# GpSimd makes the low part of each weight block in eight instructions of 256 columns in place of four of 512

## What is computed

```
h = rms_norm(x, norm1_g)
proj = h @ w_in                      # q, ckv, qi, ki, wi, u, v, ga, gb
y_a = sparse_attention(...) @ w_proj_a
y_b = chunked_gmlp(u, v, ...) @ w_proj_b
x = x + (sigmoid(ga) * y_a + sigmoid(gb) * y_b) @ w_out
x = rms_norm(x + hier_moe(rms_norm(x, norm2_g), ...))
```

```
h = x
for i in range(2):
    h = h + (dilated_mixer, forgetting_mixer)[i](rmsnorm(h, norm[i]), ...)
    h = h + swiglu(rmsnorm(h, ffn_norm[i]), w_gu[i], w_down[i])
out = rmsnorm(h, final_norm)
```

## Time and profile before

| | |
|---|---|
| timed runs | 2390.17 to 2391.84 us, median 2390.87 |
| profiled execution | 2387.72 us |
| its span, first to last instruction | 2385.9 us |
| TensorE, matmuls | busy 2263.3 us, 95% |
| TensorE, weight loads | busy 1907.7 us, 80% |
| VectorE | busy 1365.1 us, 57% |
| ScalarE | busy 1111.8 us, 47% |
| GpSimd | busy 870.3 us, 36% |
| mean granted clock of TensorE | 0.993 |

### The profile page before, as it was taken

One profiled execution on the slowest core, in us unless ns is written; L12 is line 12 of the kernel. 1 busy time (PEld: TensorE's weight loads), 2 busy tenths in 40 slices (PEclk: granted clock), 3 DMA queues, 4 the chain that ended last, 5 costly groups with the idle time before them and its releaser, 6 DMA issues.

```text
span 2385.9 us, 34966 instructions
## 1 busy us (share of the span) xinstructions
PE 2263.3 (95%) x13066; PEld 1907.7 (80%) x13066; DVE 1365.1 (57%) x2171; ACT 1111.8 (47%) x2028; POOL 870.3 (36%) x677
## 2 busy tenths in 40 slices
PE   7999999878888999999998889999999999899998
PEld 6886786545456998899987779999978887899997
DVE  4377445989885232363335687777511124977775
ACT  3344533656664344353343454444444444544443
POOL 4441241546552433333332153333132222533330
PEclk9999999999999999999999999999999999999999
DMA  5521046999994322312322123323232212233232
GB/s 182 173 71 54 36 149 240 343 392 400 392 354 161 105 89 93 103 54 71 104 79 86 36 89 108 106 95 101 89 110 86 71 54 63 80 106 96 99 107 80
DMA packets 164990, 316.68 MB, mean 133 GB/s; under 512 B 19872, under 2 KB 100512, under 8 KB 154992
## 3 DMA queue, kind: packets, MB, share of 16 engines
q1 hardware_dynamic: 157104, 301.97, 36.2%
q0 software_dynamic: 7744, 12.76, 1.6%
HBM read 300.89 MB, written 22.71 MB: 136 GB/s over the span
## 4 chain that ended last, share of the span: by engine, by line
PE 76%; DVE 8%; DMA 6%; ACT 4%; issue 4%; POOL 1%; SPq 1%; DVEq 0%; ACTq 0%; POOLq 0%
PE bank L952 21%; PE bank L954 20%; PE bank L953 20%; DMA w_ring<-in_w_gate 5%; PE bank L1578 2%; PE bank L1204 2%; PE bank L991 2%; PE bank L1183 1%; DVE up_low L2801 1%; PE bank L1555 1%; POOL w_low L3458 1%; PE bank L1194 1%; PE bank L1565 1%; PE bank L1392 1%; PE bank L1187 1%
## 5 line engine op out<-in xcount | busy, mean ns | idle before, releaser
L3458 POOL TENSOR_TENSOR w_low<-raw,w_high 128x512 fp32r<-128x512 f32 x324 | 418.1, 1321 | 820.1 <-ACT w_high L1874 788.5
L952 PE MATMUL bank<-h_high,w_high 128*128 128x256 f32 (+1 forms) x1088 | 362.7, 333 | 8.0 <-DVE h_low L2531 5.8
L954 PE MATMUL bank<-h_high,w_low 128*128 128x256 f32 (+1 forms) x1088 | 357.0, 328 | 0.0
L953 PE MATMUL bank<-h_low,w_high 128*128 128x256 f32 (+1 forms) x1088 | 356.5, 328 | 0.0
L952 PE MATMUL bank<-w_high,h_high 128*128 128x512 f32 (+2 forms) x832 | 326.5, 392 | 7.4 <-DVE h_low L2545 2.9
L954 PE MATMUL bank<-w_high,h_low 128*128 128x512 f32 (+2 forms) x832 | 311.1, 374 | 0.0
L953 PE MATMUL bank<-w_low,h_high 128*128 128x512 f32 (+2 forms) x832 | 310.9, 374 | 0.0
L952 PEld LDWEIGHTS bank<-h_high,w_high 128*128 128x128 f32 x1088 | 207.3, 191 | 31.3 <-DVE h_low L2531 10.3
L954 PEld LDWEIGHTS bank<-h_high,w_low 128*128 128x128 f32 x1088 | 207.3, 191 | 18.6
L952 PEld LDWEIGHTS bank<-w_high,h_high 128*128 128x128 f32 x832 | 204.7, 246 | 21.8 <-DVE h_low L2545 4.5
L953 PEld LDWEIGHTS bank<-h_low,w_high 128*128 128x128 f32 x1088 | 207.6, 191 | 15.5
(11 more groups left out here) (424 smaller groups left out, 4728.0 us busy)
## 6 DMA issues: line engine op xcount, KB each, us to landing
raw<-in_a_w_in SPq DMA_DIRECT2D x72, 512.0 KB, 4.6
w_ring<-in_w_gate SPq DMA_DIRECT2D x35, 1024.0 KB, 10.1
w_ring<-in_w_up SPq DMA_DIRECT2D x35, 1024.0 KB, 12.3
w_ring<-in_w_down SPq DMA_DIRECT2D x35, 1024.0 KB, 9.2
raw<-in_ffn_w_gu SPq DMA_DIRECT2D x48, 512.0 KB, 4.4
raw_more<-in_ffn_w_gu SPq DMA_DIRECT2D x40, 512.0 KB, 4.4
raw<-in_ffn_w_down SPq DMA_DIRECT2D x40, 512.0 KB, 4.4
raw<-in_w_in SPq DMA_DIRECT2D x34, 512.0 KB, 4.5
```

What stands on the lines that cost most here:

```text
L952: pe.matmul(out, sta[0], mov[0], start=start, stop=False, skip_group_check=onto)
L953: pe.matmul(out, sta[0], mov[1], start=False, stop=False, skip_group_check=onto)
L954: return pe.matmul(out, sta[1], mov[0], start=False, stop=stop, skip_group_check=onto)
L3458: last = pool.tensor_tensor(out=w_low[:, slot, cols], in0=raw[:, slot, cols], in1=w_high[:, slot, cols].bitcast(F32), op=ALU.subtract)
```

## The change

`split_low` subtracts the same 2048 columns in eight instructions of 256 columns in place of four of 512. `low_done` is still raised once, behind the last of them. `low_quarter` and the sums are not touched.

```diff
@@ -3453,8 +3453,8 @@
             pool.wait_ge(high_done, n + 1)
 
-            for q in range(4):
-                cols = slice(512 * q, 512 * q + 512)
+            for q in range(8):
+                cols = slice(256 * q, 256 * q + 256)
                 last = pool.tensor_tensor(out=w_low[:, slot, cols], in0=raw[:, slot, cols],
                                           in1=w_high[:, slot, cols].bitcast(F32), op=ALU.subtract)
             last.then_inc(low_done, 1)
```

## The result

The changed kernel takes 2395.24 us (median of 22 runs, 2390.06 to 2398.81); the kernel before takes 2390.73 us (22 runs beside them, 2385.76 to 2398.94). The ratio is 1.0019, with a 95% interval of 1.0012 to 1.0026: slower by 4.5 us, between 2.9 and 6.2. The forecast was 2395.8 us, within 2389.5 to 2400.5; the loss stands just inside the 0.2% that a measurement can tell by the forecast's bound, 4.8 us.

The account below looks back on a forecast made before the run. TensorE's work and its holes bound the kernel; GpSimd matters by latency, not throughput. Waits +7.7, queued places +1.1, VectorE's relief -3.2 and the norm -0.7 gave +4.9 on 2390.87: 2395.8 us, range 2389.5 to 2400.5.

Parts of the forecast that it names:

- The price of a start: GpSimd's split: a start costs about a one-column copy's 0.177 us, four more 0.7 us a block; bounds 0.12 and 1.4.
- rival B: Not slower by over 0.2%: VectorE's relief outweighs smaller waits; at 0.54 a block +2.2 us, 2393.1; chance 0.30.
- rival C: A start is half hidden, 0.35 us a block; sum -0.6 us, 2390.3; chance 0.15.
- The waits in the mixer: Dilated mixer: TensorE waits for each GpSimd block's added 0.7 us less its slack; 7.7 us together with places elsewhere.
- Carried along and not caught up: TensorE's delay moves ScalarE's next w_high too, so every block's added time less its slack adds to the total.
- VectorE's relief: At 34 to 39 us, three VectorE instructions wait less for shorter GpSimd instructions; 3.2 us with the clock.
- The hole: TensorE's 1.74 us idle time until 39.30 us, waiting for VectorE; forecast to shrink by 1.5 us.
- The clock's 1.7 us: Half clock from 40.3 to 43.7 us, after TensorE's idle stretch, expected to vanish, saving 1.7 us.
- The norm: Ahead of the second SwiGLU, TensorE waits for VectorE, whose waits for GpSimd shrink; relief 0.7 us.
- Queued places: Additions onto X after the experts and both SwiGLU starts: VectorE waits for GpSimd's queued work; 0.3 + 0.4 + 0.4 = 1.1 us.
- D: GpSimd loses its turn to VectorE eight times a block instead of four; +3 on the forecast, 2398.8 us; chance 0.13.
- E: Relief turns large and a start is free: faster by over 0.2%, 2386 us; chance 0.05.

Follow-up runs that it names:

- Experiments 1: Eight pieces only in the dilated mixer and its output projection, four elsewhere, against the kernel before: 2396.65 us, ratio 1.0020.
- 9: The changed kernel, but with four pieces in the dilated mixer and its output projection: 2388.90 us, ratio 0.9996 to the kernel before.
- experiment 8: Two pieces in the dilated mixer and its output projection, four elsewhere, against the kernel before: 2399.28 us, ratio 1.0037.
- Experiment 10: One piece of 2048 columns for the block at 34 us alone, against the kernel before: 2392.11 us, ratio 1.0002.
- 5: The kernel before, unchanged, profiled and timed again: 2390.29 us, ratio 0.9999.
- 6: The changed kernel, profiled and timed again: 2396.30 us, ratio 1.0023 to the kernel before.
- 11: A third profile of the changed kernel: 2392.14 us in one run.
- 2: Eight pieces for the block at 34 us alone, four elsewhere, against the kernel before: 2390.12 us, ratio 0.9996.
- 7: The kernel before with four calls of unused matmuls filling TensorE's hole at 39 us: 2391.87 us, ratio 0.9999.
- experiment 4: One piece in the dilated mixer and its output projection, eight for the block at 34 us, against the kernel before: 2426.75 us, ratio 1.0151.

## Why the prediction was right

**What bounds the kernel.** Right: POOL's throughput costs nothing and its latency at the mixer does. Experiments 1 and 9 show it from both sides, 5.5 us with eight in the mixer alone and 0.0 without. The forecast's stretch from 738 to 1345 us has grown by 5.2 us without the half clock, where some 7.5 were forecast.

**The price of a start.** Mis-sized, within its bounds: starts lie 1.246 us apart with 512 columns and 0.694 apart with 256 (medians), so a start is 2 x 0.694 - 1.246 = 0.142 us and a column 2.16 ns. The forecast took the copy's 0.177. Four starts give 0.57, and the blocks grew by 0.56, where 0.7 was forecast. The value is that of rival B (0.54), and B's +2.2 for the whole would have been 2 us too low.

The Trainium skill (GPSIMD Engine Reference, 2.1) has about 2.5 cycles per element as the floor for two inputs, which at 1.2 GHz is an estimate of 2.08 ns a column; its section 3.1, which the prediction names for that figure, has about 2.6 measured, an estimate of 2.17. The trace has 2.16. The Trainium skill (GPSIMD Engine Reference, 7) gives about 102 cycles for a small read command; taken once for each start, four more would be rival C, an estimate of 0.34 us a block. The trace has 0.56 and doesn't bear that out.

**The waits in the mixer.** Forecast 6.6 with 0.7 a block; measured 5.5. By the forecast's own count 0.56 a block gives 2.8 + 0.8 + 0.7 + 0.5 = 4.8. Matmul by matmul there are sixteen steps. The five blocks without slack give 2.8, with the one at 993 us, whose slack was 0.35: it gives 0.23, and the one at 1000 then only 0.31. The four with 0.15 and 0.23 give 0.36 to 0.39 each, 1.5 together. The four with 0.42 to 0.45 give 0.18 to 0.20 each, 0.8 together, where 0.5 would follow from their slack; blocks with 0.74 give nothing. Two steps more, 0.17 at 1035 us and 0.32 at 1074, are at no block's first load. They are a second path, which the forecast didn't have in the mixer: VectorE makes the tiny `nmx`, ScalarE waits for it and makes `dsc`, and TensorE waits for that. In the kernel before POOL's block had just ended when the second `nmx` started; the longer block still runs, and `nmx` takes 0.75 us for 0.17. First VectorE before, then VectorE and TensorE after:

```profile
1033.93 0.17 DVE L3192 TENSOR_SCALAR nmx<-msm 128x2 f32<-128x2 f32 x1
```
```profile
1035.23 0.75 DVE L3192 TENSOR_SCALAR nmx<-msm 128x2 f32<-128x2 f32 x1
...
1037.15 0.66 PE L1565 MATMUL bank<-cst,dsc 128*128 128x128 f32 x4 [0.20 <-ACT dsc L2265]
```

The two errors, the start too dear and these steps missed, went opposite ways. At 1338 us the step is 0.6 for a forecast of 0.7.

**"Carried along and not caught up."** Right: none of the sixteen steps is taken back before the second mark. Behind it 0.9 us come back, where TensorE waits for `dsc` at 1272 and 1286 us: from 1.08 + 0.80 to 0.13 + 1.36, and from 2.37 to 1.83. That is no catching up, but the same path the other way, relief on VectorE: an `nmx` that waits for the piece under way waits less for a shorter one. Before, then after:

```profile
1270.69 1.32 DVE L3192 TENSOR_SCALAR nmx<-msm 128x2 f32<-128x2 f32 x1
...
1273.36 0.17 DVE L3192 TENSOR_SCALAR nmx<-msm 128x2 f32<-128x2 f32 x1
...
1285.65 0.98 DVE L3192 TENSOR_SCALAR nmx<-msm 128x2 f32<-128x2 f32 x1
```
```profile
1275.13 0.36 DVE L3192 TENSOR_SCALAR nmx<-msm 128x2 f32<-128x2 f32 x1
...
1276.84 0.73 DVE L3192 TENSOR_SCALAR nmx<-msm 128x2 f32<-128x2 f32 x1
...
1289.70 0.45 DVE L3192 TENSOR_SCALAR nmx<-msm 128x2 f32<-128x2 f32 x1
```

The first pair gains 0.96 and loses 0.56, the third gains 0.53, and TensorE's steps are -0.4 and -0.5. In experiment 8, with pieces twice as wide, the same two waits grow by 1.0 and 1.1. The sum lacks this relief, as it lacks the loss at 1035 and 1074 us.

**VectorE's relief.** The hole shrank by 1.6 for 1.5 forecast, the three instructions at 0.67, 1.65 and 0.93 for 0.6, 1.7 and 0.9. Experiment 10 shows the mechanism with the widest instruction. The Trainium skill (SBUF, "Who interferes with whom") says that whichever of the two engines comes first holds the shared pair of ports for its whole instruction; the cast of 4.48 us agrees.

The clock's 1.7 us was forecast as certain. The profile after has it, but in the profiles of before and of experiments 1, 5, 8 and 10 the hole brings the half clock in two of five, so it is worth 0.7 us on average, as an estimate from these few. That is the step that failed, beside the path over `nmx` that was left out of the mixer; with 0.7 the sum would have been 1.0 higher.

**The norm.** Forecast -0.7, measured -0.3. The xn of 1.67 us now takes 1.13, but the two behind it went from 0.98 to 1.12 and from 1.02 to 1.30: the longer block meets more of VectorE's instructions.

**Queued places.** +0.16, +0.4 and +0.4 for +0.3, +0.4 and +0.4: right. One small thing was not seen: the block near 350 us costs 0.4, and was counted as having cover. The blocks at 105 and 325 us were given 0.2 each and cost nothing.

**The sum.** Forecast +4.9, made of +7.7 + 1.1 - 3.2 - 0.7. Measured, without the clock: +5.5 + 0.6 + 0.4 (waits), +1.0 (queued places), -0.9 (given back), -1.6 (hole), -0.3 (norm), -0.4 (at 150 and 1745 us), together +4.3; with 0.7 for the clock it is +3.6. The timed runs' interval, 2.9 to 6.2, holds both and doesn't decide. The total was nearer than its parts: the waits were forecast 1.2 too high (7.7 for 6.5) and the relief 1.3 too high (3.9 for 2.6), which cancel, and 1.3 (0.9 and 0.4) was not counted. That the sum came within 0.4 us of the measured 4.5 is in part luck.

**Rivals.** D, that POOL loses twice as many turns, came half true and cost little: the block at 34 us took 7.75 us where it took 6.67, "over 8" being the forecast of D, and the queued places have their forecast cost. E is excluded.

**What stays open.** The stretch at half clock near 1292 us. In the four profiles with eight pieces in the mixer (after, 1, 6, 11) it is there each time, with 6.8 us; in the six with four pieces (before, 2, 5, 7, 9, 10) it is missing in three, 3.4 us long in two and 6.8 in one. That looks like the change's, and would cost it up to 3 us. But the mean clock of the timed runs doesn't show it: at half clock the changed kernel spent 41.6 us (35 runs, with an error of 1.2), the kernel before 42.5 us (89 runs, 0.9), each worked out as twice the span times what the mean granted clock lacks to 1. The difference, -0.9 us with an error of 1.5, leaves room for some 2 us more at half clock, that is 1 us of time. So if the change brings on the stretch at 1292 us, it has less half clock elsewhere; whether it does wasn't settled. Not all half clock costs time either. All three profiles of the changed kernel have 3.4 us of it from 1416 to 1419 us on and again from 2064 to 2068 on, those of the kernel before have neither, and TensorE is no later for it than the 0.4 us of each SwiGLU's start.

## What to carry to other kernels

Cutting an instruction of GpSimd finer has a price for each start, 0.14 us here, that counts only where an engine waits for the last piece, and a return wherever VectorE waits for the piece under way; list both kinds of place before choosing, and choose the width by stage, since one width need not suit all. Where the waits repeat in a loop, count every place whose slack is below the added time, and then follow the tiny VectorE instructions for which another engine waits: each can gain by shorter pieces, or lose because the longer block now reaches it. A clock drop seen behind a hole in one profile is no sure gain: look at a second profile before it goes into a sum in full.

## What the runs showed of the hardware

- A tiny VectorE instruction (128x4 elements, 0.17 us alone) took up to 4.14 us beside one GpSimd subtraction of 2048 columns (4.59 us) and up to 1.93 beside one of 1024: its time is set by what is left of the other engine's instruction, not by its own size. Not every VectorE instruction waits: the reduction just ahead of it (L3191, 128x512) took 0.69 us each of its 64 times in the same run (experiment 4).
- GpSimd's subtraction, undisturbed, for 2048 columns in 1, 2, 4, 8 and 16 instructions: 4.59, 4.73, 5.00 to 5.03, 5.56 and 6.70 us, in steps of 0.14 us a start.
- The same hole of 1.74 us on TensorE was followed by 3.4 us at half clock in two profiles and by none in two others, and a hole of 3.05 us by none in the one looked at. Single times of one kernel spread over 8 to 13 us, with a standard deviation of 2.9 us (before) and 2.3 us (after), so a change below 0.1% needs more runs than were made here.
